# Two norms in halves of 256 tokens, the next stage's first tile in halves, and the squares for the next norm gathered behind the last tile

## Chip, cores and metric

One core of a Trainium2 chip runs the whole program. The metric is the device time of one execution in microseconds (us); it is 1700.46 us before the change (median of three runs).

## What is computed

Two transformer-like blocks over 512 tokens of 1024 channels, in float32. The first has a mixer (dilated attention and a spatial gating unit) and a feed-forward part; the second has two layers. The change sits at the two places in the first block where the output of a stage is normed, added to the stream, and where the new stream feeds the next stage:

```python
def rms_norm(x, g):
    y = xf * lax.rsqrt(jnp.mean(xf * xf, axis=-1, keepdims=True) + RMS_EPS)
    return (y * g.astype(jnp.float32)).astype(x.dtype)

# end of the first block's mixer, and its feed-forward part
    mix = jnp.concatenate([attn, sgu], axis=-1) @ w_out
    x = x + rms_norm(mix, g_post_mix)          # norm1, first place
    h = rms_norm(x, g_pre_ffn)                 # norm2
    f = jnp.square(jax.nn.relu(h @ w_ff1)) @ w_ff2
    return x + rms_norm(f, g_post_ffn)         # norm3, second place

# start of the second block
    hn = rmsnorm(h, norm_mix_g[layer])         # norm4
    mix = conv_pool_mixer(hn, ...)             # begins with z = hn @ cp_w_in
```

## The kernel before

Activations lie transposed, as 8 tiles (`KT`) of 128 channels by 512 tokens (`SEQ`): `xT` is the stream, `acc` the output of the stage that has just ended. Every matmul operand is split into a rounded high part and the rest (`h_hi`, `h_lo`; `whi`, `wlo`), and a product is three matmuls: high by low, low by high, high by high. Weights come in units of two tiles of 128 by 512, in a ring of four slots: SyncE loads `raw`, ScalarE writes `whi` (`split`, L1103), GpSimd writes `wlo` (L980 or L987), and TensorE waits for `unit_lo`. `split(first, j)` prepares unit `first + j + 2`.

The scale of norm2 and of norm4 (one number per token, `rs`) is applied behind the next stage's matmuls, so those need only `xT` times a gain. Norm1 and norm3 are applied ahead, and this is what stands between two stages:

1. `norm_sum(1)` or `norm_sum(3)` on TensorE adds the squares over the channels into one PSUM bank of 512 tokens (ones times `ss`, then ones times the last one or two square tiles), and `keep_clock` issues small matmuls behind it.
2. `inv_rms_in_halves` on ScalarE makes `rs` for tokens 0 to 255 (logarithm L1127, exponential L1130), then for the rest (L1131, L1134).
3. `post_normed` on VectorE goes through the tiles k = 0 to 7. Of each it makes the product with gain and `rs` (scalar_tensor_tensor, L2650), the add to `xT` (L2653), then the low part of the tile before (`lo_part`, L2603), and here and there a running sum of squares (`sum_square`, L2612 and L2615). Only of tile 0 are product and add in halves (L2640, L2643).
4. `h_parts_late_squares` on ScalarE writes the high part of each tile (L1157 for the first half of tile 0, L1160 otherwise), squares tiles (`square`, L1109) for norm2 or norm4, and splits one weight unit ahead of tile 5.
5. `unit_high_first` on TensorE takes tiles in turn: eight matmuls with the high part (L1951), then four with the low part (L1959).

There are two square tiles for this, used in turn, so that square k waits for the sum of tile k - 2. In the code before:

```python
squares = {0: (0,), 1: (1,), 4: (2,), 5: (3,), 6: (4, 5), 7: (6, 7)}   # ScalarE
sums = {3: (1,), 4: (2,), 5: (3, 4), 6: (5,), 7: (6, 7)}               # VectorE
```

A key is the tile whose high part (or low part) stands just ahead. After these eight tiles ScalarE has, in this order: the split of two units (`ffn_up(0, ..., begin=2)`; at the second place `split(U_CPIN, 2)` and `3`), at the first place four scaled copies `f` (L1365) and one more split, then `inv_rms(2)` (or `inv_rms(4)`), which reads the sum that TensorE made (`norm_sum(2)`, `norm_sum(4)`, L2012) and gives its bank back. TensorE's next matmuls (L1930) wait for the `wlo` of the first of those two units; at the first place the fourth weight column also waits for the bank that `inv_rms(2)` reads. At the second place VectorE goes on with the gates of a convolution (L3165, L3175, L3187, L3178, L3190), its taps (L3214) and, among them, four copies `upad` (L3195), each of which frees a bank of TensorE's.

Of the kernel before, what the change touches and what calls it, by code (L numbers as in the profile page):

```python
# [17 lines left out]
ALU = mybir.AluOpType  # L18
ACT = mybir.ActivationFunctionType
# [4 lines left out]
P = 128  # L24
SEQ = 512
D = 1024
# [206 lines left out]
def bank_plan():  # L233
# [14 lines left out]
    b.stage("norm1", [("sum", 0)])  # L248
# [8 lines left out]
    b.stage("norm3", [("sum", 0)])  # L257
# [19 lines left out]
def build(nc, x, w, vec, sgu_w, sgu_b, rel_bias, dw_w, pool_w, ident_c, onehot_c, lnmult_c,  # L277
# [4 lines left out]
    with ExitStack() as ctx:  # L282
# [285 lines left out]
        rs_half_log = sem("rs_half_log")  # L568
# [525 lines left out]
        def _(act):  # L1094
# [28 lines left out]
            def inv_rms_in_halves(i):  # L1123
                b = banks.bank(f"norm{i}", "sum")
                total = bank(f"norm{i}", "sum")
                act.wait_ge(filled[b], nth(f"norm{i}", "sum"))
                act.activation(rs[:, first_cols], total[:, first_cols], ACT.Ln, bias=eps6[:, :], scale=1.0 / D)\  # L1127
                    .then_inc(rs_half_log, 1)
                act.wait_ge(rs_half_log, (i + 1) // 2)
                act.activation(rs[:, first_cols], rs[:, first_cols], ACT.Exp, scale=-0.5).then_inc(rs_half, 1)  # L1130
                act.activation(rs[:, second_cols], total[:, second_cols], ACT.Ln, bias=eps6[:, :], scale=1.0 / D)\  # L1131
                    .then_inc(drained[b], 1)
                act.wait_ge(drained[b], nth(f"norm{i}", "sum"))
                act.activation(rs[:, second_cols], rs[:, second_cols], ACT.Exp, scale=-0.5).then_inc(rs_ready, 1)  # L1134
# [775 lines left out]
        def _(pe):  # L1910
# [27 lines left out]
            def unit_high_first(first, j, kts, stage, tags, n, order):  # L1938


                u = first + j
                s = u % RING
                pe.wait_ge(unit_lo, u + 1)
                for a in range(2):
                    pe.wait_ge(hi_ready, KT * n + kts[a] + 1)
                    for m in order:
                        b = banks.bank(stage, tags[m])
                        if j == 0 and a == 0:
                            pe.wait_ge(drained[b], before(stage, tags[m]))
                        for i, wt in enumerate((wlo, whi)):  # L1950
                            mm = pe.matmul(ps[:, b, :], wt[:, s, a, m * P:(m + 1) * P], h_hi[:, kts[a], :],  # L1951
                                           start=j == 0 and a == 0 and i == 0, stop=False)
                            if m == order[0] and a == 0 and i == 0:
                                mm.then_inc(unit_begun, 1)
                    pe.wait_ge(lo_ready, KT * (n - 1) + kts[a] + 1)
                    for m in order:
                        b = banks.bank(stage, tags[m])
                        last = j == 3 and a == 1
                        mm = pe.matmul(ps[:, b, :], whi[:, s, a, m * P:(m + 1) * P], h_lo[:, kts[a], :],  # L1959
                                       start=False, stop=last)  # L1960
                        if last:
                            mm.then_inc(filled[b], 1)
# [25 lines left out]
            def norm_sum(i):  # L1988
# [3 lines left out]
                if i == 1:  # L1992
                    pe.wait_ge(sq_used, KT * i - 1)
                    pe.matmul(ps[:, b, :], ones[:, :], ss[:, :], start=True, stop=False)
                    pe.wait_ge(sq_ready, KT * i)
                    pe.matmul(ps[:, b, :], ones[:, :], sq[:, 1, :], start=False, stop=True).then_inc(filled[b], 1)
                elif i == 3:
                    pe.wait_ge(sq_used, KT * i - 2)
                    pe.matmul(ps[:, b, :], ones[:, :], ss[:, :], start=True, stop=False)
                    pe.wait_ge(sq_ready, KT * i - 1)  # L2000
                    pe.matmul(ps[:, b, :], ones[:, :], sq[:, 0, :], start=False, stop=False)
                    pe.wait_ge(sq_ready, KT * i)
                    pe.matmul(ps[:, b, :], ones[:, :], sq[:, 1, :], start=False, stop=True).then_inc(filled[b], 1)
# [220 lines left out]
            pe.wait_ge(drained[3], nth("wout", ("h", 0, 3)))  # L2224
            keep_clock(3, 12)
# [81 lines left out]
            keep_clock(1, 12)  # L2307
# [282 lines left out]
        def _(dve):  # L2590
# [9 lines left out]
            def lo_part(n, k, name, off=0):  # L2600

                dve.wait_ge(hi_ready, KT * n + k + 1)
                dve.scalar_tensor_tensor(out=h_lo[:, k, :], in0=xT[:, k, :], scalar=col(name, off + k),  # L2603
                                         in1=h_hi[:, k, :].bitcast(F32), op0=ALU.mult, op1=ALU.subtract)\
# [31 lines left out]
            def post_normed(i, rs_n, gain, name):  # L2636
# [9 lines left out]
                sums = {3: (1,), 4: (2,), 5: (3, 4), 6: (5,), 7: (6, 7)}  # L2646
                for k in range(KT + 1):
# [6 lines left out]
                    if k:  # L2654
                        lo_part(i + 1, k - 1, name)
# [1186 lines left out]
```

## Time and profile before

| | |
|---|---|
| time, median of three runs | 1700.46 us (1699.83 to 1701.38) |
| the profiled execution | 1699.71 us, its span 1697.9 us |
| granted TensorE clock over the span | 1.0 |
| busy: TensorE, VectorE, ScalarE, GpSimd | 99%, 73%, 48%, 25% |
| chain that ended last, by engine | TensorE 92%, VectorE 4%, ScalarE 2%, issue 1% |

Times in the rows below are microseconds from the start of the span. A timeline row gives start, duration, engine, line, operation, output and inputs, and in brackets how long the engine was idle ahead of it and what released it. PEld is the weight load of TensorE, which overlaps its matmuls. TensorE's matmuls are pipelined: the duration of one is longer than the distance to the next. The same is true, by less, of VectorE and ScalarE.

### The profile page before, as it was taken

To read this page: it belongs to the slowest core of one execution; us is meant where nothing else is said; L and a number is where in the kernel's file an instruction comes from. 1 tells how busy PE (TensorE), PEld (TensorE's weight loads), DVE (VectorE), ACT (ScalarE), POOL (GpSimd) and SP (SyncE) were. 2 spreads that over 40 slices of the span, in tenths; PEclk is the share of its full clock that TensorE was granted. 3 is DMA by queue.
4 is the path that set the end of the run, shared out by engine and by line. 5 is a ranking of instruction groups with operands and counts; after the bars stand their busy time and mean duration, and the time that the engine had idled before them with its cause. 6 is when DMAs were issued, how large, how long until landed. Compare 5 with 4: busy or idle time off the path is not lost.

```text
span 1697.9 us, 29308 instructions
## 1 busy us (share of the span) xinstructions
PE 1685.2 (99%) x9778; PEld 1469.0 (87%) x9778; DVE 1243.0 (73%) x2272; ACT 816.0 (48%) x1425; POOL 427.9 (25%) x219
## 2 busy tenths in 40 slices
PE   9999999999999999999999999999999999999998
PEld 7877778899999788889999998888888889999997
DVE  5655569888887787688688695567675598688684
ACT  5566544333333434654353354565665554353354
POOL 3232320000001587330220204442433320220221
PEclk9999999999999999999999999999999999999999
DMA  7533213333333233223332333231212233332331
GB/s 195 124 93 92 67 58 115 96 101 99 99 99 106 74 124 95 68 94 119 112 99 87 111 100 112 75 96 53 86 62 75 62 111 108 103 126 74 99 113 50
DMA packets 159858, 162.63 MB, mean 96 GB/s; under 512 B 10627, under 2 KB 126967, under 8 KB 159775
## 3 DMA queue, kind: packets, MB, share of 16 engines
q1 hardware_dynamic: 155311, 158.66, 30.4%
q10 hardware_dynamic: 4464, 2.89, 0.6%
q8 instruction: 49, 0.80, 0.2%
q14 instruction: 34, 0.28, 0.1%
HBM read 157.84 MB, written 3.67 MB: 95 GB/s over the span
## 4 chain that ended last, share of the span: by engine, by line
PE 92%; DVE 4%; ACT 2%; issue 1%; DMA 0%; SPq 0%; DVEq 0%; ACTq 0%
PE ps L1930 36%; PE ps L2385 21%; PE ps L2410 10%; PE ps L2264 7%; PE ps L2289 6%; PE ps L2492 1%; PE ps L2328 1%; PE ps L1951 1%; PE ps L2149 1%; PE ps L2168 1%; DVE ps L3214 1%; DVE ss L2615 1%; ACT whi L1103 1%; DVE h_lo L2603 0%; PE ps L2055 0%
## 5 line engine op out<-in xcount | busy, mean ns | idle before, releaser
L987 POOL TENSOR_TENSOR wlo<-raw,whi 128x1024 fp32r<-128x1024 f32 x58 | 140.1, 2431 | 562.3 <-ACT whi L1429 292.2
L1930 PE MATMUL ps<-h_hi,wlo 128*128 128x512 f32 x608 | 247.5, 407 | 0.9 <-DVE gv L2788 0.3
L1930 PE MATMUL ps<-h_hi,whi 128*128 128x512 f32 x608 | 237.9, 391 | 0.0
L1930 PE MATMUL ps<-h_lo,whi 128*128 128x512 f32 x608 | 237.6, 391 | 0.0
L1103 ACT ACTIVATE whi<-raw 128x1024 fp32r<-128x1024 f32 x122 | 126.5, 1053 | 113.5 <-PE ps L1930 103.7
L1930 PE MATMUL ps<-m_hi,wlo 128*128 128x512 f32 x384 | 152.7, 398 | 0.0
L1930 PE MATMUL ps<-m_hi,whi 128*128 128x512 f32 x384 | 149.7, 390 | 0.0
L1930 PE MATMUL ps<-m_lo,whi 128*128 128x512 f32 x384 | 149.6, 390 | 0.0
L980 POOL TENSOR_TENSOR wlo<-raw,whi 128x1024 fp32r<-128x1024 f32 x40 | 96.9, 2428 | 192.5 <-ACT whi L1103 176.6
L1930 PEld LDWEIGHTS ps<-h_hi,whi 128*128 128x128 f32 x608 | 114.2, 188 | 25.3
L1930 PEld LDWEIGHTS ps<-h_hi,wlo 128*128 128x128 f32 x608 | 114.4, 188 | 24.8 <-POOL wlo L987 1.4
L1930 PEld LDWEIGHTS ps<-h_lo,whi 128*128 128x128 f32 x608 | 114.5, 188 | 21.2 <-issue 0.5
L1060 POOL TENSOR_TENSOR wlo<-raw,whi 128x512 fp32r<-128x512 f32 x30 | 43.2, 1474 | 355.1 <-ACT whi L1636 355.1
L3483 DVE TENSOR_TENSOR xT<-xT,ps 128x512 f32<-128x512 f32 x96 | 65.4, 686 | 86.4 <-PE ps L2410 56.6
L1628 ACT ACTIVATE whi<-wsums 128x512 fp32r<-128x512 f32 x88 | 53.4, 627 | 147.8 <-DVE wsums L3351 147.8
L1081 POOL TENSOR_TENSOR wlo<-raw,whi 128x1024 fp32r<-128x1024 f32 x28 | 68.3, 2469 | 129.3 <-ACT whi L1103 129.3
L2385 PE MATMUL ps<-h_hi,wlo 128*128 128x256 f32 x352 | 99.6, 283 | 0.0
L2385 PE MATMUL ps<-h_lo,whi 128*128 128x256 f32 x352 | 99.6, 283 | 0.0
L2385 PE MATMUL ps<-h_hi,whi 128*128 128x256 f32 x352 | 99.6, 283 | 0.0
L1930 PEld LDWEIGHTS ps<-m_hi,wlo 128*128 128x128 f32 x384 | 72.2, 188 | 15.8 <-issue 1.5
L1930 PEld LDWEIGHTS ps<-m_hi,whi 128*128 128x128 f32 x384 | 72.1, 188 | 15.1
L1930 PEld LDWEIGHTS ps<-m_lo,whi 128*128 128x128 f32 x384 | 72.2, 188 | 14.8 <-issue 0.7
(496 smaller groups left out, 4927.0 us busy)
## 6 DMA issues: line engine op xcount, KB each, us to landing
raw<-in_ffn_w SPq DMA_DIRECT2D x264, 256.0 KB, 2.9
raw<-in_w_ff SPq DMA_DIRECT2D x128, 256.0 KB, 2.8
raw<-in_hg_w_in SPq DMA_DIRECT2D x64, 256.0 KB, 3.0
raw<-in_w_in SPq DMA_DIRECT2D x40, 256.0 KB, 5.0
raw<-in_cp_w_in SPq DMA_DIRECT2D x24, 256.0 KB, 2.8
raw<-in_w_out SPq DMA_DIRECT2D x16, 256.0 KB, 3.0
raw<-in_cp_w_out SPq DMA_DIRECT2D x16, 256.0 KB, 2.9
raw<-in_hg_w_out SPq DMA_DIRECT2D x16, 256.0 KB, 2.6
```

Source lines behind the costliest of these rows:

```text
L980: pool.tensor_tensor(wlo[:, u % RING, :, :], raw[:, u % RING, :, :], whi[:, u % RING, :, :].bitcast(F32), ALU.subtract).then_inc(unit_lo, 1)
L987: pool.tensor_tensor(wlo[:, u % RING, :, :], raw[:, u % RING, :, :], whi[:, u % RING, :, :].bitcast(F32), ALU.subtract).then_inc(unit_lo, 1)
L1060: pool.tensor_tensor(lo_slot(s), raw[:, u % RING, d % 2, :], hi_slot(s).bitcast(F32), ALU.subtract)\
L1081: pool.tensor_tensor(wlo[:, u % RING, :, :], raw[:, u % RING, :, :], whi[:, u % RING, :, :].bitcast(F32), ALU.subtract).then_inc(unit_lo, 1)
L1103: act.activation(whi[:, u % RING, :, :], raw[:, u % RING, :, :], ACT.Copy).then_inc(unit_hi, 1)
L1628: act.activation(in_tiles(hi_slot(form_slot(layer, n))), form_source(layer, j, f), ACT.Copy)\
L1930: mm = pe.matmul(ps[:, b, :], wt[:, s, a, m * P:(m + 1) * P], xt[:, kts[a], :], start=starts and a == 0 and i == 0, stop=last)
L2264: mm = pe.matmul(ps[:, b, 0:HALF], wt[:, k * P:(k + 1) * P], xt[:, k, :], start=begins and TAGS[f] != "c11", stop=ends, skip_group_check=T ...
L2289: mm = pe.matmul(ps[:, 4 + m, :], wt[:, m * P:(m + 1) * P], xt[:, kt, :], start=kt == 0 and r == 0, stop=last)
L2385: mm = pe.matmul(ps[:, b, 0:HALF], wt[:, k * P:(k + 1) * P], xt[:, k, :], start=begins and TAGS[f] != "c11", stop=ends, skip_group_check=T ...
L2410: mm = pe.matmul(ps[:, 4 + m, :], wt[:, m * P:(m + 1) * P], xt[:, kt, :], start=kt == 0 and r == 0, stop=last)
L3483: dve.tensor_tensor(xT[:, k, :], xT[:, k, :], ps[:, 4 + m, :], ALU.add).then_inc(drained[4 + m], 1)
```

## The change

Norm1 and norm3 get a second bank (`rest`), so that tokens 0 to 255 are summed and released ahead of tokens 256 to 511; `keep_clock` issues 10 fp32 matmuls in place of 12. The next stage's tile 0 is multiplied in halves of 256 tokens, with two new semaphores for the first halves of its high and low part, and the low part of tile 0 is written in two instructions. Squares 4 to 7 and the sums of tiles 2 to 7 go behind the last tile's high and low part. Cut to its core:

```diff
-    b.stage("norm1", [("sum", 0)])
+    b.stage("norm1", [("sum", 0), ("rest", 3)])
-    b.stage("norm3", [("sum", 0)])
+    b.stage("norm3", [("sum", 0), ("rest", 4)])
...
             def inv_rms_in_halves(i):
+                for tag, cols, done in (("sum", first_cols, rs_half), ("rest", second_cols, rs_ready)):
+                    b = banks.bank(f"norm{i}", tag)
+                    act.wait_ge(filled[b], nth(f"norm{i}", tag))
+                    act.activation(rs[:, cols], ps[:, b, cols], ACT.Ln, bias=eps6[:, :], scale=1.0 / D)\
+                        .then_inc(drained[b], 1)
+                    act.wait_ge(drained[b], nth(f"norm{i}", tag))
+                    act.activation(rs[:, cols], rs[:, cols], ACT.Exp, scale=-0.5).then_inc(done, 1)
...
-                squares = {0: (0,), 1: (1,), 4: (2,), 5: (3,), 6: (4, 5), 7: (6, 7)}
+                squares = {0: (0,), 1: (1,), 4: (2,), 5: (3,), 7: range(4, KT)}
...
-                        act.activation(h_hi[:, 0, first_cols], xT[:, 0, first_cols], ACT.Copy, scale=vecs[:, c:c + 1])
+                        act.activation(h_hi[:, 0, first_cols], xT[:, 0, first_cols], ACT.Copy, scale=vecs[:, c:c + 1])\
+                            .then_inc(hi_half, 1)
...
+                    in_halves = j == 0 and a == 0
+                    for cols in (first_cols, second_cols) if in_halves else (slice(0, SEQ),):
+                        early = in_halves and cols == first_cols
+                        if early:
+                            pe.wait_ge(hi_half, n)
+                        else:
+                            pe.wait_ge(hi_ready, KT * n + kts[a] + 1)
+                        for m in order:
+                            for i, wt in enumerate((wlo, whi)):
+                                mm = pe.matmul(ps[:, b, cols], wt[:, s, a, m * P:(m + 1) * P], h_hi[:, kts[a], cols],
+                                               start=early and i == 0, stop=False, skip_group_check=True)
...
+                        if early:
+                            pe.wait_ge(lo_half, n)
+                        else:
+                            pe.wait_ge(lo_ready, KT * (n - 1) + kts[a] + 1)
+                        for m in order:
+                            mm = pe.matmul(ps[:, b, cols], whi[:, s, a, m * P:(m + 1) * P], h_lo[:, kts[a], cols],
+                                           start=False, stop=last, skip_group_check=True)
...
+                if i in (1, 3):
+                    halves = ((b, first_cols), (rest, second_cols))
+                    last_tiles = (1,) if i == 1 else (0, 1)
+                    pe.wait_ge(sq_used, KT * i - len(last_tiles))
+                    for bk, cols in halves:
+                        pe.matmul(ps[:, bk, cols], ones[:, :], ss[:, cols], start=True, stop=False)
+                    for t in last_tiles:
+                        pe.wait_ge(sq_ready, KT * i - 1 + t)
+                        for bk, cols in halves:
+                            mm = pe.matmul(ps[:, bk, cols], ones[:, :], sq[:, t, cols], start=False, stop=t == 1)
+                            if t == 1:
+                                mm.then_inc(filled[bk], 1)
...
-            pe.wait_ge(drained[3], nth("wout", ("h", 0, 3)))
-            keep_clock(3, 12)
+            pe.wait_ge(drained[4], nth("wout", ("h", 1, 0)))
+            keep_clock(4, 10)
...
-            keep_clock(1, 12)
+            keep_clock(1, 10)
...
-                sums = {3: (1,), 4: (2,), 5: (3, 4), 6: (5,), 7: (6, 7)}
+                sums = {3: (1,), 7: range(2, KT)}
...
-                    if k:
-                        lo_part(i + 1, k - 1, name)
+                    if k == 0:
+                        dve.wait_ge(hi_half, i + 1)
+                        dve.scalar_tensor_tensor(out=h_lo[:, 0, first_cols], in0=xT[:, 0, first_cols], scalar=col(name, 0),
+                                                 in1=h_hi[:, 0, first_cols].bitcast(F32), op0=ALU.mult, op1=ALU.subtract)\
+                            .then_inc(lo_half, 1)
+                    else:
+                        lo_part(i + 1, k - 1, name, cols=slice(0, SEQ) if k > 1 else second_cols)
```

## Rows read from the trace of the kernel before

**Rows 1.** Windows: busy us and count by engine, granted clock, DMA share.

```profile
233.00:255.00 22.00, 21.91 (x97) 18.15 (x98) 20.14 (x29) 13.04 (x20) 4.39 (x2) 1.00 0.08 25
```

**Rows 2.** Timeline of the first place, from the sum to the first product.

```profile
228.51 1.02 PE L1996 MATMUL ps<-sq,ones 128*128 128x512 f32 x2
...
231.63 0.51 ACT L1157 ACTIVATE h_hi<-xT,vecs 128x256 fp32r<-128x256 f32 x1 [0.32 <-DVE xT L2643]
...
232.37 0.75 DVE L2650 SCALAR_TENSOR_TENSOR acc<-acc,vecs,rs 128x512 f32<-128x512 f32 x1
...
233.09 0.47 PE L1951 MATMUL ps<-h_hi,wlo 128*128 128x512 f32 x1 [0.88 <-issue]
```

**Rows 3.** The chain that ended last: start, us, what (512 and 256 columns).

```profile
258.12 63.56 PE ps L1930 x279
...
850.04 40.31 PE ps L2385 x336
```

**Rows 4.** The page's costliest groups, the one with 256 columns.

```profile
L2385 PE MATMUL ps<-h_hi,wlo 128*128 128x256 f32 x352 | 99.6, 283 | 0.0
```

**Rows 5.** Timeline of VectorE, first place, tiles 4 to 7.

```profile
240.57 0.68 DVE L2612 TENSOR_TENSOR ss<-sq,ps 128x512 f32<-128x512 f32 x1
241.17 0.74 DVE L2650 SCALAR_TENSOR_TENSOR acc<-acc,vecs,rs 128x512 f32<-128x512 f32 x1
...
242.56 0.74 DVE L2603 SCALAR_TENSOR_TENSOR h_lo<-xT,vecs,h_hi 128x512 fp32r<-128x512 f32 x1
243.22 0.68 DVE L2615 TENSOR_TENSOR ss<-ss,ps 128x512 f32<-128x512 f32 x1
243.81 2.29 DVE L2650 SCALAR_TENSOR_TENSOR acc<-acc,vecs,rs 128x512 f32<-128x512 f32 x1
...
251.45 0.74 DVE L2603 SCALAR_TENSOR_TENSOR h_lo<-xT,vecs,h_hi 128x512 fp32r<-128x512 f32 x1
252.12 1.47 DVE L2615 TENSOR_TENSOR ss<-ss,ps 128x512 f32<-128x512 f32 x2
```

**Rows 6.** Timeline of GpSimd, first place.

```profile
242.94 2.61 POOL L980 TENSOR_TENSOR wlo<-raw,whi 128x1024 fp32r<-128x1024 f32 x1 [17.12 <-ACT whi L1103]
253.23 4.76 POOL L987 TENSOR_TENSOR wlo<-raw,whi 128x1024 fp32r<-128x1024 f32 x2 [7.67 <-ACT whi L1103]
```

**Rows 7.** Timeline of ScalarE and TensorE, first place, end of the tiles.

```profile
250.94 1.23 ACT L1109 ACTIVATE ps<-xT 128x512 f32<-128x512 f32 x2
...
252.11 1.99 ACT L1103 ACTIVATE whi<-raw 128x1024 fp32r<-128x1024 f32 x2
...
254.98 1.02 PE L2012 MATMUL ps<-ss,ones 128*128 128x512 f32 x2
255.68 0.19 PEld L1930 LDWEIGHTS ps<-h_hi,wlo 128*128 128x128 f32 x1 [0.51 <-POOL wlo L987]
...
258.12 0.19 PEld L1930 LDWEIGHTS ps<-h_hi,wlo 128*128 128x128 f32 x1 [0.47 <-ACT rs L1114]
```

**Rows 8.** Timeline of the second place.

```profile
579.79 0.47 PE L1951 MATMUL ps<-h_hi,wlo 128*128 128x512 f32 x1 [0.87 <-issue]
...
602.41 0.53 PE L1930 MATMUL ps<-h_hi,wlo 128*128 128x512 f32 x1
602.75 0.69 ACT L1114 ACTIVATE rs<-ps,eps 128x512 f32<-128x512 f32 x1 [1.91 <-PE ps L2012]
...
605.13 2.41 POOL L987 TENSOR_TENSOR wlo<-raw,whi 128x1024 fp32r<-128x1024 f32 x1 [0.41 <-ACT whi L1103]
...
607.10 1.40 DVE L3187 TENSOR_TENSOR staged<-staged,csig 128x512 f32<-128x512 f32 x1 [0.64 <-ACT csig L1495]
```

**Rows 9.** Timeline of VectorE and TensorE further on, second place.

```profile
609.13 2.35 DVE L3190 TENSOR_TENSOR apad<-apad,csig 128x512 f32<-128x512 f32 x1
...
625.47 0.39 PE L1930 MATMUL ps<-h_hi,whi 128*128 128x512 f32 x1
626.08 0.50 PE L1930 MATMUL ps<-h_hi,wlo 128*128 128x512 f32 x1 [0.22 <-DVE upad L3195]
```

More of the change, by code:

```diff
@@ L567, in build @@
         rs_half = sem("rs_half")
-        rs_half_log = sem("rs_half_log")
+        hi_half = sem("hi_half")
+        lo_half = sem("lo_half")
         post_half = sem("post_half")
@@ L1123, in inv_rms_in_halves @@
             def inv_rms_in_halves(i):
[L1124 to L1134, printed above, removed]
+                for tag, cols, done in (("sum", first_cols, rs_half), ("rest", second_cols, rs_ready)):
[5 more added lines that the diff above has]
+                    act.activation(rs[:, cols], rs[:, cols], ACT.Exp, scale=-0.5).then_inc(done, 1)
             def h_parts(n, i, ready, name, off=0, units={}):
@@ L1944, in unit_high_first @@
                 for a in range(2):
[L1945 to L1962, printed above, removed]
+                    in_halves = j == 0 and a == 0
@@ new lines, in unit_high_first @@
+                    for cols in (first_cols, second_cols) if in_halves else (slice(0, SEQ),):
[5 more added lines that the diff above has]
+                        for m in order:
+                            b = banks.bank(stage, tags[m])
+                            if early:
+                                pe.wait_ge(drained[b], before(stage, tags[m]))
+                            for i, wt in enumerate((wlo, whi)):
+                                mm = pe.matmul(ps[:, b, cols], wt[:, s, a, m * P:(m + 1) * P], h_hi[:, kts[a], cols],
+                                               start=early and i == 0, stop=False, skip_group_check=True)
+                                if m == order[0] and a == 0 and i == 0 and (early or j):
+                                    mm.then_inc(unit_begun, 1)
+                        if early:
+                            pe.wait_ge(lo_half, n)
+                        else:
+                            pe.wait_ge(lo_ready, KT * (n - 1) + kts[a] + 1)
+                        for m in order:
+                            b = banks.bank(stage, tags[m])
+                            last = j == 3 and a == 1
+                            mm = pe.matmul(ps[:, b, cols], whi[:, s, a, m * P:(m + 1) * P], h_lo[:, kts[a], cols],
+                                           start=False, stop=last, skip_group_check=True)
+                            if last:
+                                mm.then_inc(filled[b], 1)
@@ L1991, in norm_sum @@
                 pe.wait_ge(drained[b], before(f"norm{i}", "sum"))
[L1992 to L2003, printed above, removed]
+                if i in (1, 3):
+                    rest = banks.bank(f"norm{i}", "rest")
+                    pe.wait_ge(drained[rest], before(f"norm{i}", "rest"))
+                    halves = ((b, first_cols), (rest, second_cols))
[9 more added lines that the diff above has]
+                                mm.then_inc(filled[bk], 1)
                 elif i >= 5:
@@ L2598, in col, with lo_part @@
                 return vecs[:, COL[name] + k:COL[name] + k + 1]
-            def lo_part(n, k, name, off=0):
+            def lo_part(n, k, name, off=0, cols=slice(0, SEQ)):
                 dve.wait_ge(hi_ready, KT * n + k + 1)
-                dve.scalar_tensor_tensor(out=h_lo[:, k, :], in0=xT[:, k, :], scalar=col(name, off + k),
-                                         in1=h_hi[:, k, :].bitcast(F32), op0=ALU.mult, op1=ALU.subtract)\
+                dve.scalar_tensor_tensor(out=h_lo[:, k, cols], in0=xT[:, k, cols], scalar=col(name, off + k),
+                                         in1=h_hi[:, k, cols].bitcast(F32), op0=ALU.mult, op1=ALU.subtract)\
                     .then_inc(lo_ready, 1)
```

## The prediction

> **What bounds the kernel now.** I read the page first: TensorE is busy 99% of the span and carries 92% of the chain that ended last. A change that adds no matmul work can therefore only move the few places where TensorE waits. Next I read the chain and the timeline around the two places of the change. At the first place TensorE waits 0.88 us and begins the new stage at 233.09, as soon as the high part of tile 0 is whole [rows 2]. From there on it works through the eight tiles without a gap: it is busy 21.91 of 22.00 us, while VectorE is busy 20.14 [rows 1]. So TensorE and VectorE are both nearly full here, and one has to ask which of them sets the end. The end of the place gives the answer. TensorE begins the first ordinary unit at 255.68 after 0.51 us of waiting for GpSimd's `wlo`, and is stopped once more until 258.12, by the bank that ScalarE's L1114 gives back [rows 7]. Both come from ScalarE's order of work: last square, then split, split, and so on from 252.11. Behind 258.12 comes a chain of 279 matmuls at 0.228 us [rows 3], and the timeline shows no wait worth naming up to the second place. The end of this place is thus set by when ScalarE is through with square 7, not by when TensorE begins.
>
> The second place is the same code, 346.7 us later (579.79 against 233.09) [rows 2, 8]. There the same split and `wlo` release TensorE at 602.41. Then there are two paths to 626.08: TensorE's own matmuls, which have a slack of 0.61 - 0.23 = 0.38 us (distance of the last two rows, less one pitch), and VectorE's gates and taps, behind ScalarE's L1114 at 602.75 [rows 8, 9].
>
> **The change part by part, first place.** All estimates here are worked out from the rows.
>
> *Sum in halves.* An fp32 matmul of 512 columns is two passes, together 1.02 us [rows 2]. A matmul lasts some 0.16 longer than its pitch (0.39 against 0.228) [rows 3, 9], so a pass takes (1.02 - 0.16) / 2 = 0.43, and one of 256 columns half of that. The two passes over tokens 256 to 511, 0.43 us together, no longer stand ahead of the release of tokens 0 to 255; a few ns per extra pass come off that. I take 0.40 us. It carries over to ScalarE's and VectorE's first halves unchanged. The smaller `keep_clock` ends earlier by about the same, so it holds nothing up.
>
> *First tile in halves.* TensorE can begin when the high part's first half is written: L1157 ends at 232.14 [rows 2], less 0.40, plus the 0.09 that TensorE needed before, gives 231.83 (1.26 us earlier). A 512-column matmul has a pitch of 63.56 / 279 = 0.228, as have the 96 from 233.09 to 254.98 [rows 2, 7]; a 256-column one has 40.31 / 336 = 0.120 [rows 3, 4]. So tile 0 costs 24 x 0.120 = 2.88 in place of 12 x 0.228 = 2.74 us. The second half of its low part stands behind product and add of tile 1 and holds TensorE some 0.07. Tile 1 begins at 231.83 + 2.88 + 0.07 = 234.78 where it began at 235.83. Nothing later is late: the tightest is the low part of tile 5, ready at about 247.3 and wanted at 247.6. TensorE would be through the eight tiles at 253.93 instead of 254.98, 1.05 us early.
>
> *One more instruction on VectorE.* The low part's first half takes 0.40 of pitch. It eats the 0.40: the product of tile 1 starts at 232.37 as before [rows 2]; the second half of the low part is shorter than the whole by 0.26, so from tile 2 on VectorE is 0.26 early.
>
> *Sums moved behind the last low part.* This decides. Between tiles a sum costs 0.60 of pitch (240.57 to 241.17) [rows 5]. Chained one behind another each waits for the one before: two take 1.47, a pitch of 0.78. Worse, one sum was free. GpSimd's 2.61 us at 242.94 [rows 6] holds up VectorE's product, 2.29 us for 0.74, and the sum at 243.22 ran under it in its usual 0.68 [rows 5]. After the change the product of tile 6 stands there directly. It would still end 0.55 us after GpSimd does, as now (245.55 and 246.10), so at 245.84. Then, with the usual pitches (product and add 1.39 together, 241.17 to 242.56, of which the product has 0.78; low part 0.66): add of tile 6 at 245.88, low 5 at 246.49, product 7 at 247.15, add 7 at 247.93, low 6 at 248.54; the high part of tile 7 is written by 249.38, low 7 runs from 249.42 (before 251.45) [rows 5]. Now six sums: 250.09, 250.87, 251.65, 252.43, 253.21, 253.99, the last done at 254.68. Square 7 waits for the sum of tile 5, done at 253.12, starts at 253.16, and the split follows 0.54 later at 253.70, where it stood at 252.11 [rows 7]: 1.59 us later.
>
> *What is late next.* Queued behind square 7 on ScalarE are the two splits, the four copies, one split, L1114. GpSimd's first `wlo` ends at 257.22, TensorE's first ordinary unit begins at 257.28 and its stop at the bank ends at 259.71, each 1.59 later than in [rows 7]. TensorE itself is ready early: it waits 0.8 us from 253.93 for the last sum, then again for `wlo`. Since the chain behind has no slack [rows 3], the 1.59 us stay.
>
> On the block of VectorE by GpSimd: the row shows VectorE's product waiting and the sum from PSUM not [rows 5, 6]. The Trainium skill, "SBUF — State Buffer", section "Who interferes with whom", says that whichever issues first gets the shared port pair for the whole instruction, and that a VectorE instruction with at most one SBUF input does not contend; the trace agrees. By this rule the order matters: if the product of tile 6 comes first, GpSimd waits and the add is held instead. Worked out from the rows, GpSimd then starts some 0.6 later and the add of tile 6 ends at about 246.45 instead of 246.57, so either order gives the same sum within 0.1 us.
>
> **Second place.** The same 1.59, with 0.02 of rounding, moves TensorE's unit from 602.41 to 604.02. Its slack of 0.38 comes off: 1.23 at 626.08 [rows 8, 9]. The other path: the last sum is done at 601.4, L1114 at 602.50 is 0.25 early. But GpSimd now does its units from 601.56 to 606.3 and the next one until 608.7 (before from 605.13, 2.41), so L3187 is held until about 609.64 (before 608.50), then L3190 waits for the next unit and ends at 612.55 (before 611.48), 1.07 late [rows 8, 9]. VectorE would free the bank at 627.15, TensorE arrives at 627.31; the larger counts: 1.23 us.
>
> **Sum.** 1.59 + 1.23 = 2.8 us. On the profiled execution (span 1697.9, time 1699.71) that is a span of 1700.7 and 1702.5 us; that execution lies 0.75 below the median of the runs, and on the median I forecast 1703.3 us. The bound for a difference that a measurement of this kernel can tell is 0.2%, 3.4 us; the forecast is slower by 0.17%, just inside.
>
> **Bounds of what the trace does not show.** A chained sum could cost 0.60 (as between tiles) to 0.78: up to 0.7 us less per place. The hold of the product of tile 6 could be none (an instruction of 0.74) up to the whole 2.40 plus 0.55: up to 2.1 less. The second place's VectorE path could lose one GpSimd instruction more, 2.4 less the little slack: up to 2.2 more. Half passes and half matmuls are seen at other shapes and can hardly be off by 0.2 in total.
>
> **Rivals.**
> - *The sums stay hidden.* If the product of tile 6 isn't held, VectorE is 2.1 us earlier: sum 5 is done at 251.0, the split is at 251.6, 0.5 early, and TensorE gains 0.5 at the first place and about as much at the second: 1699.4 us. It decides from the point where square 7 starts before 251.57. For it speaks that TensorE then has its 1.05 us; against it that GpSimd's instruction is released by the same sum of tile 1 and so moves with VectorE. Even the full 1.05 twice would give 1698.4, not faster by 0.2%. To be that, the clock or another stage must change, for which no row speaks.
> - *The start of the stage sets the end.* Then both places give their 1.05, less what the second place's path takes: 1698.4 to 1699.4. The two waits in [rows 7] speak against it.
> - *The convolution's path takes the lead at the second place.* GpSimd's units come in a closer row and L3187 and L3190 each meet one; if one more is met, VectorE frees the bank 2.2 us later than I reckon, 3.3 in place of 1.23: 1705.4 us.
> - *The change is neutral* because both ends are held by something I don't see: 1700.5.
>
> **Chances.** Forecast as worked out (1702.3 to 1704.3): 0.55. Sums hidden: 0.12; start sets the end: 0.05; convolution path: 0.15; neutral: 0.08; the rest, 0.05, anything else. The range that leaves out 2 in 10: 1700.3 to 1705.0. Slower by over 0.2% (over 1703.9) holds the convolution path and a part of the forecast's upper side: 0.25; faster by over 0.2%: 0.03; within 0.2%: 0.72.
>
> **What would show it.** TensorE's first half-width matmul at about 231.8 and tile 1 at 234.8; a VectorE product of over 2.5 us at tile 6; six sums in a row behind the last low part, from about 250.1; TensorE idle twice around `norm_sum(2)`; split at 253.7 instead of 252.11; first ordinary unit at 257.3 instead of 255.7; and the same 346.7 + 1.6 us later. I am wrong if the split stands at 252.1 or before, or if the product of tile 6 takes 0.75.

## The result, and the profile after

The changed kernel takes 1704.08 us (median of 15 runs, 1702.38 to 1705.22); the kernel before took 1699.86 us (15 runs, 1699.43 to 1701.38; three of them gave the 1700.46 on which I forecast). The ratio is 1.0024, 95% interval 1.0017 to 1.0031: slower by 4.2 us. I had forecast 2.8 us more and a range up to 1705.0. The profiled execution took 1704.58 us, its span 1702.8 us (before 1697.9), at a mean clock of 0.998.

The page, busy time by engine and the chain that ended last by engine:

```profile
PE 1686.3 (99%) x9804; PEld 1471.8 (86%) x9804; DVE 1247.8 (73%) x2274; ACT 816.5 (48%) x1425; POOL 428.2 (25%) x219
...
PE 92%; DVE 4%; ACT 2%; DMA 1%; issue 1%; POOL 0%; ACTq 0%; SPq 0%; DVEq 0%
```

The shares are those of before, but for one: DMA has 1% of the chain, where the page before has 0%. The difference comes from three transfers behind the convolution of the second place (*Second place*, below). For the rest one has to go to the windows. Columns: busy us and count of TensorE, weight load, VectorE, ScalarE, GpSimd; granted clock; DMA share; GB/s.

```profile
233.00:255.00 22.00, 21.22 (x101) 17.58 (x100) 20.73 (x29) 11.27 (x18) 2.89 (x2) 1.00 0.07 24
...
257.20:260.60 3.40, 3.40 (x9) 2.63 (x10) 2.52 (x4) 3.37 (x6) 2.22 (x1) 0.52 0.49 161
```

The first row answers to [rows 1]: TensorE is now idle for 0.78 us of it. The second row has a granted clock of 0.52, near the lower level of 1.2 GHz, and it begins right behind the two waits of TensorE around `norm_sum(2)`. Here are those waits and the start of the place, TensorE's timeline (answers to [rows 2, 7]):

```profile
227.50 1.10 PE L2006 MATMUL ps<-ss,ones 128*128 128x256 f32 x4 [0.18 <-DVE ss L2624]
...
231.74 0.36 PE L1955 MATMUL ps<-h_hi,wlo 128*128 128x256 f32 x1
...
234.76 0.40 PE L1955 MATMUL ps<-h_hi,wlo 128*128 128x512 f32 x1
...
254.77 1.10 PE L2021 MATMUL ps<-ss,ones 128*128 128x512 f32 x2 [0.78 <-DVE ss L2624]
...
257.13 0.66 PE L1928 MATMUL ps<-h_hi,wlo 128*128 128x512 f32 x1 [1.27 <-POOL wlo L988]
...
259.29 0.63 PE L1928 MATMUL ps<-h_hi,whi 128*128 128x512 f32 x1
259.72 0.63 PE L1928 MATMUL ps<-h_hi,wlo 128*128 128x512 f32 x1
...
260.88 0.39 PE L1928 MATMUL ps<-h_hi,wlo 128*128 128x512 f32 x1
```

TensorE starts the stage at 231.74 in place of 233.09, works through it without a gap, and then gives all of it back: 0.78 us waiting for VectorE's last sum, 1.27 us for `wlo`. Behind these waits the matmuls of 512 columns start 0.43 us apart (259.29 to 259.72), where they start 0.228 apart at the upper level of 2.4 GHz; from 260.88 on they are fast again. VectorE, which is where this comes from (answers to [rows 5]):

```profile
242.85 2.88 DVE L2659 SCALAR_TENSOR_TENSOR acc<-acc,vecs,rs 128x512 f32<-128x512 f32 x1
...
249.97 4.65 DVE L2624 TENSOR_TENSOR ss<-ss,ps 128x512 f32<-128x512 f32 x6
```

And ScalarE's split, which waits for the square before it, with GpSimd's answer (answers to [rows 6, 7]):

```profile
253.61 1.99 ACT L1104 ACTIVATE whi<-raw 128x1024 fp32r<-128x1024 f32 x2
...
254.72 4.69 POOL L988 TENSOR_TENSOR wlo<-raw,whi 128x1024 fp32r<-128x1024 f32 x2 [9.54 <-ACT whi L1104]
```

The second place shows the same two waits and no drop of the clock (1.00 from 600 to 614), and one more wait 75 us behind them (answers to [rows 8]):

```profile
576.06 1.10 PE L2006 MATMUL ps<-ss,ones 128*128 128x256 f32 x4
...
604.18 1.10 PE L2021 MATMUL ps<-ss,ones 128*128 128x512 f32 x2 [0.75 <-DVE ss L2624]
...
606.59 0.50 PE L1928 MATMUL ps<-h_hi,wlo 128*128 128x512 f32 x1 [1.31 <-POOL wlo L988]
...
609.66 2.53 DVE L3201 TENSOR_TENSOR staged<-staged,csig 128x512 f32<-128x512 f32 x1 [0.64 <-ACT csig L1493]
...
650.24 8.20 PE L2337 MATMUL ps<-blocks,first_table 128*128 128x128 f32 x72
...
679.39 1.10 PE L2363 MATMUL ps<-csum,ones 128*128 128x512 f32 x2 [1.31 <-DVE csum L3267]
```

The same marks in the kernel before, where the mean matmul (the last row) has no wait:

```profile
227.58 1.10 PE L1994 MATMUL ps<-ss,ones 128*128 128x512 f32 x2 [0.18 <-DVE ss L2615]
...
573.43 1.10 PE L1999 MATMUL ps<-ss,ones 128*128 128x512 f32 x2
...
646.64 8.20 PE L2328 MATMUL ps<-blocks,first_table 128*128 128x128 f32 x72
...
674.45 1.10 PE L2354 MATMUL ps<-csum,ones 128*128 128x512 f32 x2
```

Distances between these marks cut the span into pieces that can be compared from run to run. *Start* is where the sum of norm1 begins; *first* is from there to the sum of norm3 (573.43 - 227.58 = 345.85 before); *to conv* is from there to the first convolution matmul (73.21); *to mean* is also from norm3's sum, to the mean matmul (101.02). All are in us and of one profiled execution for each kernel.

| kernel | start | first | to conv | to mean | span |
|---|---|---|---|---|---|
| before | 227.58 | 345.85 | 73.21 | 101.02 | 1697.9 |
| changed | 227.50 | 348.56 | 74.18 | 103.33 | 1702.8 |
| changed, run again (e8) | 227.71 | 348.41 | 74.24 | 103.51 | 1703.1 |
| halves only (e1) | 227.98 | 345.55 | 72.70 | 101.52 | 1698.7 |
| late squares only (e2) | 226.83 | 347.72 | 74.47 | 102.28 | 1700.2 |
| busy waits (e3) | 227.92 | 347.43 | 74.23 | 102.39 | 1701.1 |
| late squares at the first place only (e7) | 228.89 | 347.44 | 72.74 | 101.32 | 1701.1 |
| sums under GpSimd (e4) | 227.66 | 344.42 | 72.13 | 100.93 | 1696.5 |
| the same again (e10) | 229.03 | 344.44 | 72.13 | 100.84 | 1697.6 |
| the same without halves (e5) | 226.91 | 345.49 | 73.19 | 101.01 | 1696.8 |
| split ahead of squares (e6) | 226.98 | 345.68 | 73.33 | 102.15 | 1698.3 |
| mean later (e9) | 228.99 | 344.43 | 72.11 | 101.16 | 1697.4 |

In the last row the mean matmul itself stands behind six more matmuls of the output product, so its *to mean* can't be compared with the others. What lies behind the mean is the same in before and changed within 0.05 us. So the 4.9 us of span are 2.71 at the first place and 2.31 at the second (less 0.08 of a different start). The start, ahead of all edits, itself varies between 226.8 and 229.0, which is why the spans alone can't be compared to a microsecond, and the pieces can. Part of that goes with the clock at the very beginning: in the first 20 us it was 1.00 in before, e2, e5 and e6, which start at 226.8 to 227.6, and 0.91 in all others, which start at 227.5 to 229.0. A mean clock of 0.998 over an execution is therefore no sign of the drop at the first place.

### The profile page after: what moved, and what is told of

Its sections match the earlier page's. It is cut to its first block, busy times and chain, and to the rows that moved or that the text cites. A ratio compares the mean times of both kernels' runs of the same rounds, so it can differ in the third digit from the quotient of the medians.

```text
span 1702.8 us, 29370 instructions
## 1 busy us (share of the span) xinstructions
PE 1686.3 (99%) x9804; PEld 1471.8 (86%) x9804; DVE 1247.8 (73%) x2274; ACT 816.5 (48%) x1425; POOL 428.2 (25%) x219
## 4 chain that ended last, share of the span: by engine, by line
PE 92%; DVE 4%; ACT 2%; DMA 1%; issue 1%; POOL 0%; ACTq 0%; SPq 0%; DVEq 0%
PE ps L1928 38%; PE ps L2394 21%; PE ps L2419 10%; PE ps L2273 7%; PE ps L2298 6%; PE ps L2501 1%; DVE acc L2659 1%; PE ps L2158 1%; PE ps L2177 1%; DVE xT L2662 1%; DVE ss L2624 0%; PE ps L2337 0%; DVE h_lo L2612 0%; PE ps L2064 0%; PE ps L2070 0%
```

## The experiments

None of them leaves out a part of the computation. The theory: the late sums and squares delay the split, and the halves are worth little without them. The rivals: the halves themselves cost (short matmuls, more instructions); the clock, and not the queue, makes the loss.

**e1: the halves, with squares and sums where they were.**

```diff
-                squares = {0: (0,), 1: (1,), 4: (2,), 5: (3,), 7: range(4, KT)}
+                squares = {0: (0,), 1: (1,), 4: (2,), 5: (3,), 6: (4, 5), 7: (6, 7)}
-                sums = {3: (1,), 7: range(2, KT)}
+                sums = {3: (1,), 4: (2,), 5: (3, 4), 6: (5,), 7: (6, 7)}
```

> The changed kernel with the squares and sums between the tiles as before; only the halves (norm sums, first tile) are left of the change. Theory: what costs time is the row of late sums, and the end of each place is set by ScalarE's first split behind square 7. Then the split stands at about 251.85 (0.26 before the 252.11 of before), TensorE is not idle before the next norm's sum, the clock stays at 1.0, and the time is 0.2 to 0.9 us under before. Rival 1, the halves themselves cost (more passes, 24 small matmuls for 12): 2 to 4 us over before. Rival 2, the start of the stage sets the end: 2 us under before.

Measured: 1700.45 us against 1699.74, ratio 1.0003 (0.9994 to 1.0012): no difference. That rules out 2 us less (the start sets the end) and nearly all of the 2 to 4 us more (the halves cost); the 0.2 to 0.9 us less of the theory did not show in the time. ScalarE and TensorE at the end of the first place:

```profile
252.23 1.99 ACT L1104 ACTIVATE whi<-raw 128x1024 fp32r<-128x1024 f32 x2
```

```profile
255.79 0.19 PEld L1928 LDWEIGHTS ps<-h_hi,wlo 128*128 128x128 f32 x1 [0.70 <-POOL wlo L988]
...
258.24 0.19 PEld L1928 LDWEIGHTS ps<-h_hi,wlo 128*128 128x128 f32 x1 [0.53 <-ACT rs L1115]
```

This execution started 0.40 late, so the split is 0.28 early against before's, and the first place gains 0.30. TensorE's start, more than a microsecond earlier, turns into waiting for `wlo` and for the bank. The second place is 0.51 early at the convolution, and then loses 1.01 up to the mean, where TensorE waits 1.0 us for `csum`. The halves cost nothing where they stand, and what they gain there is lost again further on.

**e2: the other part alone; the same two lines changed the other way, in the kernel before.**

```diff
-                squares = {0: (0,), 1: (1,), 4: (2,), 5: (3,), 6: (4, 5), 7: (6, 7)}
+                squares = {0: (0,), 1: (1,), 4: (2,), 5: (3,), 7: range(4, KT)}
-                sums = {3: (1,), 4: (2,), 5: (3, 4), 6: (5,), 7: (6, 7)}
+                sums = {3: (1,), 7: range(2, KT)}
```

> The kernel before with squares 4 to 7 and sums 2 to 7 behind the last tile; no halves. Theory: VectorE lacks the 0.26 us of the halves, so the first split stands at about 253.9, 1.8 us late at the first place, the same at the second, and the time is 3 to 4.5 us over before. TensorE's waits fall behind the norm's sum, 1.5 to 1.8 us in one piece. Rival 1 (the halves cost): the time of before within 0.5 us.

Measured: 1703.32 us, ratio 1.0021 (1.0012 to 1.0030), 3.6 us over before, as the theory has it. The split at the first place (this execution started 0.75 early), and TensorE's waits for `wlo` behind 200 us (total us, count, longest):

```profile
253.22 1.99 ACT L1103 ACTIVATE whi<-raw 128x1024 fp32r<-128x1024 f32 x2
```

```profile
PE ps L1930 <- POOL wlo L987: 2.6, 2, 1.3
```

From the sum of norm1 the split is 126.39 away, before it was 252.11 - 227.58 = 124.53: 1.86 later, and the piece of the first place is 1.87 longer. The delay passes to the end of the place one for one, with no halves in the kernel and the clock at its upper level. The second place loses 1.26 at the convolution and still 1.26 at the mean. So this part alone makes 3.13 of the 5.02 us that the two places lose in the changed kernel's profile, and TensorE's wait is 1.3 us at each place, a little less than the 1.5 to 1.8 expected.

**e3: the change, with small matmuls that fill the two waits.**

```diff
+            pe.wait_ge(drained[0], before("ffnup", ("m", 0), 0))
+            keep_clock(0, 3)
             norm_sum(2)
+            keep_clock(0, 5)
...
+            pe.wait_ge(drained[4], before("cpin", ("g", 2, 0)))
+            keep_clock(4, 3)
             norm_sum(4)
+            keep_clock(4, 5)
```

> The changed kernel with small fp32 matmuls on TensorE where it was idle: 3 ahead of norm_sum(2) and norm_sum(4), 5 behind them. Nothing else moves. Theory: late sums cost 1.6 at the first place and about 1 at the second, and the clock, which fell to half at the first place after the two idle waits, adds some 1.2 to that. Then the granted clock is 1.0 from 257.2 to 260.6, the tenth ordinary matmul starts at 259.6 to 259.8 and not at 260.9, and the time is about 1.2 us under the changed kernel, 3 over before. Rival 2, the clock is the whole loss: the time of before. Rival 3, the clock hides behind the bank that L1115 gives back: the time of the changed kernel.

```profile
250.00:262.00 12.00, 11.58 (x56) 8.95 (x55) 7.99 (x12) 9.89 (x14) 4.72 (x2) 1.00 0.22 71
```

In this window of the profiled execution TensorE is nearly always busy and the clock stays at 1.00. The first place comes out at 347.43, which is 1.58 over before: the whole queue's delay, and the clock's part of 2.71 gone. But the median of the five runs is 1706.52 (ratio 1.0037, 1.0023 to 1.0051), not 1.2 us under the changed kernel as expected. Two runs lie at 1703.65 and 1703.70, the profiled one among them, and three at 1706.52 to 1707.34, over every run of the changed kernel. In four of the five the device time is 2.46 to 2.60 us longer than the span, in all runs of the other kernels it is 1.75 to 1.89: some 0.7 us lies outside the span, where no row is. The rest of the slower runs' time has no profile. So the one profile bears out what the clock costs at the first place; that filling the waits helps the kernel is not shown, and since the two intervals overlap, neither is that it harms it.

**e7: the late squares and sums at the first place alone.**

```diff
-                squares = {0: (0,), 1: (1,), 4: (2,), 5: (3,), 7: range(4, KT)}
+                squares = {..., 5: (3,), 7: range(4, KT)} if i == 2 else {..., 5: (3,), 6: (4, 5), 7: (6, 7)}
-                sums = {3: (1,), 7: range(2, KT)}
+                sums = {3: (1,), 7: range(2, KT)} if i == 0 else {3: (1,), 4: (2,), 5: (3, 4), 6: (5,), 7: (6, 7)}
```

> The changed kernel with late squares and sums at the first place only; at the second they stand between the tiles as before, halves at both. Theory: the first place keeps its whole loss, 2.6 us with the clock, the second gains 0.2 to 0.5, and the time is 2.0 to 2.6 us over before. If the second place were the main loss, the time would be under 1.5 us over before.

Measured: 1701.43 us, 1.69 over before, ratio 1.0012 (1.0003 to 1.0021). That lies under the 2.0 us that I expected at least, and the profile shows a reason. TensorE, and the window behind its two waits:

```profile
256.18 1.10 PE L2021 MATMUL ps<-ss,ones 128*128 128x512 f32 x2 [0.80 <-DVE ss L2624]
258.54 0.50 PE L1928 MATMUL ps<-h_hi,wlo 128*128 128x512 f32 x1 [1.27 <-POOL wlo L988]
...
261.03 0.50 PE L1928 MATMUL ps<-h_hi,wlo 128*128 128x512 f32 x1 [0.15 <-ACT rs L1115]
```

```profile
258.00:262.00 4.00, 3.31 (x13) 2.45 (x14) 2.51 (x4) 3.97 (x7) 2.86 (x2) 1.00 0.43 137
```

The waits are those of the changed kernel (0.80, and 1.27 for `wlo`), but the clock is 1.00 here. The first place costs 347.44 - 345.85 = 1.59 us. The prediction had worked out the same number; that it agrees to the hundredth is luck, that it agrees to a tenth is not, since every step in between does. Behind the waits nine matmuls and a wait for the bank take 2.49 us here (258.54 to 261.03); in the changed kernel's profile nine slow matmuls alone take 3.75 (257.13 to 260.88). Of these 1.26 us 0.14 is back by norm3's sum. What the clock adds there is then 2.71 - 1.59 = 1.12 us.

**e8: the changed kernel again, unaltered.**

> The changed kernel unaltered, for a second profile on this chip. Open is whether the half clock behind the idle waits (257 to 260.6) is in every execution. If so, the tenth ordinary matmul stands 33.4 us behind the start of the norm's sum again; if not, 32.1. The time is 3 to 5 us over before in either case.

```profile
250.00:262.00 12.00, 9.94 (x35) 7.19 (x34) 7.98 (x12) 9.90 (x14) 4.68 (x2) 0.86 0.25 79
```

1703.57 us, ratio 1.0024 (1.0014 to 1.0034), and the clock falls at the same place (0.86 over this window); the first place is 2.56 longer, 0.97 of it over the 1.59. So the drop is no accident of one execution. At the changed kernel's second place the same two waits go by with no drop in either profile, and in e2 one wait of 1.3 at each place. In how many of the runs without a profile the clock falls is not known.

**e4: the halves, with the sums where GpSimd's instruction covers them.** The product of tile 6 costs 2.88 us because it is held; sums would not be. So three sums go ahead of it, to the place where GpSimd is at work.

```diff
-                squares = {0: (0,), 1: (1,), 4: (2,), 5: (3,), 7: range(4, KT)}
+                squares = {0: (0,), 1: (1,), 4: (2,), 5: (3, 4), 6: (5,), 7: (6, 7)}
-                sums = {3: (1,), 7: range(2, KT)}
+                sums = {3: (1,), 4: (2, 3, 4), 6: (5,), 7: (6, 7)}
```

> The changed kernel with the halves kept, but sums of tiles 2, 3 and 4 in a row behind the low part of tile 4, where GpSimd's wlo holds VectorE's product, and sums 5, 6 and 7 spread behind tiles 6 and 7 (square 4 behind tile 5, square 5 behind tile 6). Theory: VectorE's sums read one operand from PSUM and run under GpSimd for nothing, so three of them cost no more than the hold of 2.3 us. Then the first split stands about 1.6 us earlier than before the change, TensorE waits neither for wlo nor for the bank, the first place gains 1.0 to 1.3 us and the second up to 1.0 more, less what the convolution's transfers take back: time 1.2 to 2.2 us under before. Rival: sums are held by GpSimd like the products; then the time is 1 to 2 us over before.

```profile
243.02 2.26 DVE L2624 TENSOR_TENSOR ss<-ss,ps 128x512 f32<-128x512 f32 x3
...
245.20 0.75 DVE L2659 SCALAR_TENSOR_TENSOR acc<-acc,vecs,rs 128x512 f32<-128x512 f32 x1
...
242.74 2.63 POOL L981 TENSOR_TENSOR wlo<-raw,whi 128x1024 fp32r<-128x1024 f32 x1 [16.84 <-ACT whi L1104]
...
250.55 2.00 ACT L1104 ACTIVATE whi<-raw 128x1024 fp32r<-128x1024 f32 x2
```

```profile
250.00:262.00 12.00, 12.00 (x53) 9.57 (x52) 8.79 (x15) 9.16 (x12) 4.76 (x2) 1.00 0.28 89
```

Three sums run in 2.26 us under GpSimd's 2.63, and the product behind them takes 0.75 in place of 2.88. The split is at 250.55, from the sum of norm1 1.64 earlier than before the change, and TensorE has no idle time between 250 and 262. The Trainium skill, "SBUF — State Buffer", section "Who interferes with whom", says that a VectorE instruction with at most one input in SBUF, outside the modes that use two ports, does not contend with GpSimd. The trace agrees, as these sums have one input in SBUF and one in PSUM and keep the pitch of chained sums, 0.79 us. The first place gains 1.43. At the second the convolution stands 1.08 earlier behind norm3's sum, but only 0.09 of that is left at the mean, where TensorE waits 0.95 for `csum`. Measured: 1698.54 us, ratio 0.9993 (0.9984 to 1.0002).

**e10: e4 again**, beside e9.

> e4_sums_under_wlo unaltered, to sharpen its comparison and for a second profile. Theory: 1.2 to 1.6 us under before again, with the clock at full between the end of the tiles and the first ordinary unit; rival: the first result was a lucky start, and it is the time of before.

1697.94 us, ratio 0.9990 (0.9981 to 0.9999), the same pieces within 0.1 us. Together with e4: 1.3 and 1.9 us less than before. e10's interval lies just under 1, e4's reaches over it; both are less than the 0.2% that the prediction takes as the least difference to be told.

**e5: the same order of squares and sums in the kernel before, without halves.**

```diff
-                squares = {0: (0,), 1: (1,), 4: (2,), 5: (3,), 6: (4, 5), 7: (6, 7)}
+                squares = {0: (0,), 1: (1,), 4: (2,), 5: (3, 4), 6: (5,), 7: (6, 7)}
-                sums = {3: (1,), 4: (2,), 5: (3, 4), 6: (5,), 7: (6, 7)}
+                sums = {3: (1,), 4: (2, 3, 4), 6: (5,), 7: (6, 7)}
```

> The same order of squares and sums in the kernel before, without halves. Theory: now TensorE's own 96 matmuls set the end of each place, so of the 1.4 us that VectorE gains only the 0.2 to 0.5 of the two short waits is worth anything: time 0.2 to 0.7 us under before. Rival, VectorE sets the end alone: 1.4 us or more under before.

```profile
254.29 1.02 PE L2012 MATMUL ps<-ss,ones 128*128 128x512 f32 x2
...
254.72 0.19 PEld L1930 LDWEIGHTS ps<-h_hi,wlo 128*128 128x128 f32 x1 [0.24 <-issue]
```

Measured: 1699.57 us, ratio 0.9998 (0.9989 to 1.0007). The wait for `wlo` is gone, but TensorE now arrives with its own work at its own time, and the first place gains only 0.36. Halves alone gain 0.30 (e1), the order alone 0.36 (e5), both 1.43 (e4). With halves alone the end is held by the split, which is 0.28 earlier; with the order alone by TensorE's own matmuls (254.29 - 226.91 = 127.38 us from the sum of norm1 to that of norm2, before 127.40). That is the gain which the changed kernel could not collect.

**e6: the change, with both splits ahead of the late squares on ScalarE.**

```diff
                     act.activation(h_hi[:, k, cols], xT[:, k, cols], ACT.Copy, scale=vecs[:, c:c + 1]).then_inc(hi_ready, 1)
+                    if k == KT - 1:
+                        split(first, 2)
+                        split(first, 3)
                     for s in squares.get(k, ()):
...
-            ffn_up(0, 0, 0, 0, begin=2, middle=scaled_and_norm)
+            ffn_up(0, 0, 0, 0, begin=4, middle=scaled_and_norm)
...
-            for j in range(2, 4):
-                split(U_CPIN, j)
             inv_rms(4)
```

> The changed kernel with late squares and sums, but the two splits of ScalarE ahead of squares 4 to 7. Theory: what makes late sums costly is what is queued behind square 7. With wlo ready by 252.8, TensorE waits only for the last sum (about 0.9 us) and no longer for wlo; the tenth ordinary matmul stands within 0.5 us of that of before, at both places nearly all of the loss is gone, and the time is from 0.3 under to 0.7 us over before. Rival, the last sum itself is the loss: 2 us or more over before.

```profile
248.66 2.00 ACT L1104 ACTIVATE whi<-raw 128x1024 fp32r<-128x1024 f32 x2
```

```profile
254.39 1.10 PE L2022 MATMUL ps<-ss,ones 128*128 128x512 f32 x2 [0.92 <-DVE ss L2625]
```

Measured: 1700.68 us, ratio 1.0007 (0.9998 to 1.0016), against 1.0024 with the splits behind. The late sums are as they were, and TensorE still waits 0.92 us for the last of them, but the wait for `wlo` has gone, and the first place is 0.17 shorter than before. So the loss at the first place is what stood behind the squares on ScalarE; the sums themselves hold TensorE by those 0.92 us, of the microsecond that its earlier start had won. The second place is 0.12 longer up to the convolution and 1.13 up to the mean; the loss behind the convolution stays.

**e9: e4, with the mean's matmul later among the output products.**

```diff
-            cpout(1, slice(0, 4))
+            cpout(1, slice(0, 6))
...
-            cpout(1, slice(4, 8))
+            cpout(1, slice(6, 8))
```

> e4_sums_under_wlo, with six small matmuls of the output product (1.4 us) moved from behind the convolution's mean to ahead of it, into TensorE's wait for csum. Theory: with the halves, that wait of about 1 us is a real loss of TensorE's time, because the convolution's round trip through memory has become the last to arrive. Then the wait vanishes, the sum of squares behind it, which had about 1 us to spare, takes at most 0.4 of that back, and the time is 0.5 to 1.0 us under e4. Rival: the wait only moves to the variance's matmul; the time of e4 within 0.3 us.

```profile
682.92 1.10 PE L2370 MATMUL ps<-csum,ones 128*128 128x512 f32 x2 [0.48 <-DVE csum L2760]
```

Measured: 1697.80 us, ratio 0.9988 (0.9979 to 0.9997), 0.14 us under e10 and so no different from it: the rival. TensorE waited 0.87 us at the mean in e10; here it waits 0.48 at the matmul of the variance. That matmul stands 0.46 earlier behind norm3's sum (109.50 us against 109.96), of which 0.15 is left at the end of the span. Against before it is 2.0 us, as with e10 a small gain with an interval just under 1.

## Why the prediction was right, and by how much it missed

**What bounds the place.** Right. The start on TensorE moved 1.35 us and the end did not follow; in e1, with the same early start, the first place gains 0.30, about what its split is earlier (0.28).

**Sum and tile in halves.** Right: 231.83 forecast, 231.74 seen; tile 1 at 234.78, seen 234.76. (Tile 1 began at 235.93 in the trace before, where I had reckoned 235.83; nothing rests on it.)

**Sums behind the last low part.** Right, step for step, and this is the shown cause of the loss at the first place (e2, e6, e7). The product of tile 6 was forecast to start directly behind and be held over 2.5 us: 2.88. The sums: 250.09 forecast, 249.97 seen, six in 4.65 us. The split: 253.70, seen 253.61. The first ordinary unit: 257.28, seen 257.13. The first place's 1.59 us is what e7 measures without a drop of the clock, and e3's profile shows 1.58; e2, without halves, has 1.87.

**The clock.** Missing from the sum. I had named it only in one rival, as something that would have to change for a gain and for which no row speaks. It fell behind the two waits in both profiles of the changed kernel, which cost 1.12 and 0.97 us. I forecast these two waits and did not price them beyond their length.

**Second place.** The term of 1.23 us was mis-sized; 2.31 was measured. The path that I had worked out is there: the first ordinary unit is 1.55 late, L3201 is held (2.53 us), L3204 behind it is 0.90 late (forecast 1.07), and up to the convolution the loss is 0.97. In e2, which has the late squares without the halves, it is 1.26 at the convolution and still 1.26 at the mean, near the forecast of 1.23. The other 1.34 of the changed kernel come between convolution and mean, where I had not looked. My rival put a further loss on the path through gates and taps, with 3.3 us in place of 1.23, and named the wrong wait: it is not a GpSimd instruction more, but the round trips of the convolution's output through memory. There are two of them, one for each tile of 128 channels: ScalarE stores (`conv_phases<-staged`), waits until that is done, loads in another order (`blocks<-conv_phases`), and adds a bias (`conv`), on which the mean rests. ScalarE with its queue, in the changed kernel and then in the kernel before:

```profile
659.10 0.35 ACTq L1511 DMA_DIRECT2D conv_phases<-staged  x1
...
663.50 1.78 ACTq L1520 DMA_DIRECT2D blocks<-conv_phases  x4
...
670.92 0.34 ACTq L1511 DMA_DIRECT2D conv_phases<-staged  x1
...
672.96 1.76 ACTq L1520 DMA_DIRECT2D blocks<-conv_phases  x4
677.24 1.20 ACT L1526 ACTIVATE conv<-blocks,vecs 128x512 f32<-128x512 f32 x1 [4.81 <-DMA blocks<-conv_phases]
```

```profile
655.50 0.35 ACTq L1513 DMA_DIRECT2D conv_phases<-staged  x1
...
657.87 1.76 ACTq L1522 DMA_DIRECT2D blocks<-conv_phases  x4
...
666.35 0.60 ACT L1511 ACTIVATE staged<-ps 128x512 f32<-128x512 f32 x1 [1.53 <-PE ps L2328]
666.98 0.34 ACTq L1513 DMA_DIRECT2D conv_phases<-staged  x1
...
669.01 1.76 ACTq L1522 DMA_DIRECT2D blocks<-conv_phases  x4
672.29 1.21 ACT L1528 ACTIVATE conv<-blocks,vecs 128x512 f32<-128x512 f32 x1 [3.81 <-DMA blocks<-conv_phases]
```

From norm3's sum the first store is issued 0.97 later (83.04 against 82.07) and takes 4.40 us in place of 2.37, so that its reload is 3.00 later (87.44 against 84.44). Of this 1.69 is absorbed, mainly by the 1.53 us for which ScalarE had waited for TensorE ahead of the second store; that store is 1.31 later. Its own duration is the same (2.04 and 2.03 us), but from its reload to the activation behind it 4.28 us pass in place of 3.28. The activation is 2.32 later (101.18 against 98.86), which is the loss at the mean: 0.97 from the convolution, 0.34 through the first trip, 1.00 in the second reload.

All twelve profiles can be read for this. From the second reload to its activation it is 3.28 to 3.30 us in the three kernels without halves (before, e2, e5), and 3.50 to 4.30 in the nine profiles with halves, e10 with 3.52 and e4, the same kernel, with 4.28. The first store takes 2.4 us in some of those with halves (e3, e6, e7) and 4.0 to 4.8 in the others. From the first store to the last activation it is 16.79 to 16.81 us without halves and 17.15 to 18.26 with them. So the halves go with this cost of 0.4 to 1.5 us; by what way is not shown. It also took the gain at the second place from e1 and e4.

**The sum.** 1.59 + 1.23 = 2.82 forecast; 1.59 + 1.12 (clock) + 0.97 + 1.34 (mean), with 0.13 less for start and the rest, are the 4.9 us between the spans; the medians differ by 4.2. The mechanism at the first place was right; the size was too small because the clock and the trips behind the convolution had no term. That 1704.08 us lies within the 1702.3 to 1704.3 of the forecast itself is luck: this band is 1.8 to 3.8 us over the three runs from which I started, the loss is 4.2 us, and the median of fifteen runs before is 0.6 us under that of the three. In the wider range it lies only because that was stretched for a rival with another wait. The measured 0.24% lies over the 0.2% under which I had put the likeliest case.

**The rivals.** The sums don't stay hidden (split 1.59 late), the start doesn't set the end (e1), and nothing is neutral. e4 shows the first of them to be a matter of place: with the sums under GpSimd's instruction they do hide.

## What to carry to other kernels

When work that can wait is moved behind the last tile of a stage, read what is queued behind it on each engine: here the last squares waited for chained sums, and behind those, in order, stood the weight split on which the next stage's matmuls wait. An earlier start of a full engine is worth nothing until the wait at its end is moved too; test both together, since here each alone gave 0.3 to 0.4 us and both gave 1.4. Before instructions are moved, see under what they run: a sum with an operand in PSUM was free beside GpSimd, and the product that took its place was held for 2.88 us. Then follow a gain or loss up to the next round trip through memory, which may take it back or add to it.

## What was not expected of the hardware

- The granted clock fell to 0.52 for 3.4 us behind two waits of 0.78 and 1.27 us in one profile of the changed kernel, and fell at the same place in its second, but not in e7 behind waits of 0.80 and 1.27, nor at the second place with 0.75 and 1.31. What decides between them the runs don't show.
- Small matmuls in those waits kept the clock at 1.00 in the profile, and the median of that kernel was no lower all the same: two of five runs near 1703.7 and three from 1706.5 to 1707.3, and in four of them 0.7 us more than usual between the span and the device time.
- The first store from `staged`, of the same size everywhere, took 2.4 us in six profiles and 4.0 to 4.8 in the other six, and 4.0 and 4.8 in two profiles of the same kernel (e4, e10). The second took 2.0 in all of them.
